# Expert jobs of a hybrid diffusion kernel: the next job's token rows fetched by an indirect DMA in place of gather products

## What is computed

```python
def moe_swiglu(h, w_router, b_router, w_gate, w_up, w_down):
    t = h.reshape(bsz * t_len, dm)
    logits = (t @ w_router).astype(jnp.float32) + b_router.astype(jnp.float32)
    top_v, top_i = lax.top_k(logits, TOP_K)                  # 2 of 8
    top_p = jax.nn.softmax(top_v, axis=-1)
    comb = jnp.sum(jax.nn.one_hot(top_i, N_EXPERTS) * top_p[..., None], axis=1)
    y = jnp.zeros_like(t)
    for e in range(N_EXPERTS):
        y = y + comb[:, e:e + 1] * swiglu(t, w_gate[e], w_up[e], w_down[e])   # width 1408
```

## Time and profile before

| | |
|---|---|
| median of 3 runs | 1898.19 us |
| lowest, highest | 1896.22, 1906.67 us |
| the profiled execution, its own time | 1911.24 us |
| its span, first to last instruction | 1909.3 us |
| PE busy | 1778.1 us, 93% |
| DVE busy | 1130.6 us, 59% |
| ACT busy | 902.9 us, 47% |
| POOL busy | 556.3 us, 29% |
| DMA | 315.33 MB, mean 165 GB/s |
| mean granted clock of PE | 0.97 of 2.4 GHz |

### The profile page before, as it was taken

The page is one execution under the profiler, slowest core; times in us unless marked ns, Lnnn a source line. Parts: engine busy times, 40 slices in busy tenths (PEclk is TensorE's granted clock), DMA queues, the critical chain, the costliest instruction groups (busy, mean ns, idle before and its releaser), DMA issues.

```text
span 1909.3 us, 40982 instructions
## 1 busy us (share of the span) xinstructions
PE 1778.1 (93%) x16558; PEld 1628.1 (85%) x16558; DVE 1130.6 (59%) x1623; ACT 902.9 (47%) x1358; POOL 556.3 (29%) x423
## 2 busy tenths in 40 slices
PE   7898989899999999989988899999899999999996
PEld 6896868799999999989968788999788878888885
DVE  2365688754331111033666885532589888889987
ACT  3335242243344333333441423434567777777765
POOL 1560000265566666656600003656300000000000
PEclk9998989999999999989999999999999999999998
DMA  8446141233423444423571101336388999899880
GB/s 286 153 135 225 48 130 60 82 117 116 154 78 122 133 133 133 125 86 106 162 229 60 33 4 32 111 127 217 133 312 296 297 316 310 308 316 316 291 286 34
DMA packets 225286, 315.33 MB, mean 165 GB/s; under 512 B 15734, under 2 KB 169716, under 8 KB 225012
## 3 DMA queue, kind: packets, MB, share of 16 engines
q1 hardware_dynamic: 217856, 306.22, 48.8%
q10 hardware_dynamic: 7284, 6.97, 1.2%
HBM read 311.05 MB, written 2.10 MB: 164 GB/s over the span
## 4 chain that ended last, share of the span: by engine, by line
PE 78%; DVE 11%; issue 4%; ACT 4%; DMA 1%; ACTq 1%; DVEq 0%; POOL 0%; SPq 0%
PE bank L598 76%; PE bank L595 2%; DVE e_w_rest L186 2%; DVE S L1981 2%; DMA ring<-in_w_ada 1%; ACT e_w_rounded L1354 1%; DVE cvT L1884 1%; DVE hg_rest L1785 1%; DVE St L2033 0%; DVE U L2011 0%; DVE hT L1753 0%; DVE St L2030 0%; DVE hT L1734 0%; DVE tmp L1899 0%; DVE ey_rest L2291 0%
## 5 line engine op out<-in xcount | busy, mean ns | idle before, releaser
L2384 POOL TENSOR_TENSOR weights_rest<-ring,weights_rounded 128x512 fp32r<-128x512 f32 x344 | 467.4, 1362 | 457.7 <-ACT weights_rounded L1317 456.9
L186 DVE TENSOR_TENSOR e_w_rest<-e_raw,e_w_rounded 128x1024 fp32r<-128x1024 f32 (+1 forms) x326 | 353.7, 1132 | 35.0 <-ACT e_w_rounded L1354 33.8
L1317 ACT ACTIVATE weights_rounded<-ring 128x512 fp32r<-128x512 f32 x344 | 215.5, 629 | 335.1 <-PE bank L598 322.3
L1354 ACT ACTIVATE e_w_rounded<-e_raw 128x1024 fp32r<-128x1024 f32 (+1 forms) x327 | 315.2, 989 | 80.8 <-PE bank L598 80.2
L598 PE MATMUL bank<-h_rounded,weights_rounded 128*128 128x384 f32 x688 | 234.4, 341 | 12.4 <-DVE h_rest L1785 4.9
L598 PE MATMUL bank<-h_rest,weights_rounded 128*128 128x384 f32 x688 | 232.2, 338 | 0.0
L598 PE MATMUL bank<-h_rounded,weights_rest 128*128 128x384 f32 x688 | 232.2, 337 | 0.0
L598 PE MATMUL bank<-e_w_rounded,hG_rounded 128*128 128x512 f32 (+1 forms) x432 | 164.5, 381 | 6.7 <-DVE hG_rest L2283 3.5
L598 PE MATMUL bank<-e_w_rest,hG_rounded 128*128 128x512 f32 (+1 forms) x432 | 162.7, 377 | 0.0
L598 PE MATMUL bank<-e_w_rounded,hG_rest 128*128 128x512 f32 (+1 forms) x432 | 162.7, 377 | 0.0
L598 PEld LDWEIGHTS bank<-h_rounded,weights_rounded 128*128 128x128 f32 x688 | 131.1, 191 | 16.7 <-issue 6.0
(11 more groups left out here) (350 smaller groups left out, 3615.4 us busy)
## 6 DMA issues: line engine op xcount, KB each, us to landing
ring<-in_w_ada SPq DMA_DIRECT2D x96, 512.0 KB, 6.2
e_raw<-in_moe_w_down SPq DMA_DIRECT2D x90, 512.0 KB, 4.6
ring<-in_w_in SPq DMA_DIRECT2D x88, 512.0 KB, 4.5
e_raw<-in_moe_w_gate SPq DMA_DIRECT2D x72, 512.0 KB, 5.6
e_raw<-in_moe_w_up SPq DMA_DIRECT2D x72, 512.0 KB, 6.6
e_raw<-in_moe_w_gate SPq DMA_DIRECT2D x36, 384.0 KB, 3.8
e_raw<-in_moe_w_up SPq DMA_DIRECT2D x36, 384.0 KB, 3.9
ring<-in_ffn_w_gate SPq DMA_DIRECT2D x22, 512.0 KB, 4.6
```

The costliest lines, as they stand in the source:

```text
L186: eng.tensor_tensor(wl, e_raw[n % E_RAW][:, 0:kn * w], wr.bitcast(F32), ALU.subtract).then_inc(s("e_rest"), 1)
L1317: a(w_parts[n % NSLOT][0], raw, ACT.Copy).then_inc(*E.up("rounded_ready", *key))
L1354: a(e_w[n % E_PARTS][0][:, 0:kn * w], e_raw[n % E_RAW][:, 0:kn * w], ACT.Copy).then_inc(s("e_rounded"), 1)
L2384: pool.tensor_tensor(wl, raw, wr.bitcast(F32), ALU.subtract).then_inc(*E.up("rest_ready", *key))
```

## The change

The next job's rows are no longer multiplied together on PE. Before the loop POOL adds the two parts of the token rows and stores the sums, 1.5 MB, to device memory (h_rows). In each job, the token numbers ride along with the mixing weights as a second column of wsel; the product with sel gives for each slot its weight and its row number. DVE copies both out of bank 5 (slot_values: rows_at, wnext), and POOL issues an indirect DMA that fetches the 128 rows to hgt. PE waits for it ahead of the transposes behind piece 31.

For this DVE selects earlier, behind the rest of piece 19 (SELECT_AT = 20), and the small product with wsel (slot_rows) moves on PE from before piece 16 to behind piece 20. As the down products overwrite bank 5, PE waits at piece 24 for the copies (e_rows_at). hgt gets a place of its own; the first job still uses gather products. The weight buffers start at a fixed column, 88 further on than before.

```diff
-GATHER_AT, GATHERED_AT = 29, 31
+SELECT_AT, SLOTS_AT, ROWS_AT, GATHERED_AT = 20, 20, 27, 31
...
+E_RAW_AT = 25640
...
+    out["token"] = i[:, None] + P * np.arange(4)[None, :]
...
+            def slot_rows(i):
+                pe.wait_ge(s("e_wsel"), i + 1)
                 for j in range(3):
-                    last = mm(psum[5][:, 0:1], sel[:, j, :].bitcast(F32), wsel[:, j:j + 1], j == 0, j == 2)
-                last.then_inc(s("e_selT_full"), 1)
+                    last = mm(psum[5][:, 0:2], sel[:, j, :].bitcast(F32), wsel[:, j, :], j == 0, j == 2)
+                last.then_inc(s("e_slot_full"), 1)
...
-            turn_gathered(0)
+            turn_gathered(True)
+            slot_rows(0)
...
+                        if n == SLOTS_AT:
+                            slot_rows(i + 1)
...
                     if k0 == 0:
                         pe.wait_ge(s("e_selT"), i * 2 + 2)
+                        pe.wait_ge(s("e_rows_at"), i + 2)
...
-                    if n == GATHER_AT:
-                        pe.wait_ge(s("e_sel"), i + 2)
-                        for h in range(2):
-                            for part in range(2):
-                                gather(h, part)
-                    elif n == GATHERED_AT:
-                        turn_gathered(i + 1)
+                    if n == GATHERED_AT:
+                        pe.wait_ge(s("e_rows_in"), i * 16 + 16)
+                        turn_gathered(False)
...
-                        a(wslot, psum[5][:, 0:1], ACT.Copy).then_inc(s("e_selT"), 1)
+                        act.wait_ge(s("e_rows_at"), i + 1)
+                        a(wslot, wnext, ACT.Copy).then_inc(s("e_selT"), 1)
...
-                e_round(i, done + 4, GATHER_AT + E_PARTS)
-                e_gathered(i + 1)
-                e_round(i, GATHER_AT + E_PARTS, GATHERED_AT + E_PARTS)
+                e_round(i, done + 4, GATHERED_AT + E_PARTS)
...
-            select_weights(lambda at_: slice(at_, at_ + 1))
+            dve.tensor_copy(wsel[:, :, 1], tab("token")[:, 0:3]).then_inc(*E.step())
+            select_weights(lambda at_: slice(at_, at_ + 1)).then_inc(s("e_wsel"), 1)
...
+            def slot_values(i):
+                dve.wait_ge(s("e_slot_full"), i + 1)
+                dve.tensor_copy(rows_at, psum[5][:, 1:2])
+                dve.tensor_copy(wnext, psum[5][:, 0:1]).then_inc(s("e_rows_at"), 1)
+
+            slot_values(0)
...
+                    if c == 2:
+                        e_rests(i, done, SELECT_AT)
+                        dve.wait_ge(s("e_selT_full"), i + 1)
+                        code = dve.value_load(rt_i[0:1, bass.ds(i + 19, 1)], min_val=0, max_val=NCODE - 1)
+                        select_slots(lambda at_: bass.ds(code + at_, 1))
+                        select_weights(lambda at_: bass.ds(code + at_, 1)).then_inc(s("e_wsel"), 1)
+                        done = SELECT_AT
...
-                    if c == 2:
-                        dve.wait_ge(s("e_selT_full"), i + 1)
-                        code = dve.value_load(rt_i[0:1, bass.ds(i + 19, 1)], min_val=0, max_val=NCODE - 1)
-                        select_slots(lambda at_: bass.ds(code + at_, 1))
-                        select_weights(lambda at_: bass.ds(code + at_, 1)).then_inc(s("e_sel"), 1)
+                dve.wait_ge(s("e_selT"), i * 2 + 2)
+                slot_values(i + 1)
                 e_rests(i, done, done + 4)
...
+            pool.wait_ge(s("e_gather"), 2)
+            for j in range(3):
+                pool.tensor_tensor(h_sums[:, j, :], hT_parts[0][:, j, :].bitcast(F32), hT_parts[1][:, j, :].bitcast(F32), ALU.add)\
+                    .then_inc(*E.up("row_summed"))
+                pool.wait_ge(*at("row_summed"))
+                pool.dma_start(h_rows[j * P:(j + 1) * P, :], h_sums[:, j, :]).then_inc(*E.up("rows_stored", by=16))
+            pool.wait_ge(*at("rows_stored"))
+            pool.wait_ge(*at("jobs_ready"))
+            njobs = pool.value_load(rt_i[0:1, 0:1], min_val=NE, max_val=NJOB)
+            with pool.Fori(0, njobs) as i:
+                pool.wait_ge(s("e_rows_at"), i + 2)
+                pool.wait_ge(s("e_hT_full"), i * 2 + 2)
+                pool.sem_inc(s("e_rows_go"), 1)
+                pool.indirect_dma_start(hgt, None, h_rows, bass.IndirectOffsetOnAxis(rows_at, 0))\
+                    .then_inc(s("e_rows_in"), 16)
```

More of the change, by code:

```diff
@@ L94, in tables @@
     return {k: np.asarray(v, np.float32) for k, v in out.items()}
-FIRST = ("ident", "ones", "before", "iota", "code", "eps")
+FIRST = ("ident", "ones", "before", "iota", "code", "token", "eps")
 def table_columns():
@@ L309, in build @@
         htok = cut("htok", o, 3 * DM).rearrange("p (j d) -> p j d", j=3)
-        hT_parts = parts("htoken", DM, 3, o, o + 3 * DM); o += 6 * DM
+        hT_parts = parts("htoken", DM, 3, o, o + 3 * DM)
+        h_sums = cut("h_sums", o, 3 * DM).rearrange("p (j d) -> p j d", j=3)
+        hgt = cut("hgt", o + 3 * DM, DM); o += 6 * DM
         hG = parts("hG", P, KD, o, o + DM); o += 2 * DM
         eprod = cut("eprod", o, DE); o += DE
-        hgt = cut("hgt", used["eprod"][0], DM)
+        hgt0 = cut("hgt0", used["eprod"][0], DM)
         ey = [p_[:, 0, :] for p_ in parts("ey", DM, 1, o, o + DM)]; o += 2 * DM
@@ L316, in build @@
         sel, selT = parts("sel", P, 3, o, o + 3 * P); o += 6 * P
-        wsel = cut("wsel", o, 3); o += 3
+        wsel = cut("wsel", o, 6).rearrange("p (j w) -> p j w", w=2); o += 6
         wslot = cut("wslot", o, 1); o += 1
+        wnext = cut("wnext", o, 1); o += 1
+        rows_at = cut("rows_at", o, 1).bitcast(I32); o += 1
         esig = cut("esig", o, 512); o += 512
@@ L325, in build @@
         fin_row = cut("fin_row", o, DM); o += DM
-        o = (o + 7) // 8 * 8
+        assert o <= E_RAW_AT
+        o = E_RAW_AT
         e_raw = [cut(f"e_raw{i}", o + i * DM, DM) for i in range(E_RAW)]; o += E_RAW * DM
@@ L359, in gsig @@
             return tmp4[3 if i % 8 >= 4 else 0][:, (i % 4) * T:(i % 4 + 1) * T]
+        h_rows = nc.dram_tensor("h_rows", [T, DM], F32, kind="Internal").ap()
         sems = {}
@@ L1140, in gather, with turn_gathered @@
                     last.then_inc(s("e_gather"), 1)
-            def turn_gathered(i):
+            def turn_gathered(first):
                 for h in range(2):
-                    pe.wait_ge(s("e_hgt"), i * 2 + h + 1)
+                    if first:
+                        pe.wait_ge(s("e_hgt"), h + 1)
                     for k in range(4):
-                        last = transpose(psum[h][:, k * P:(k + 1) * P], hgt[:, (4 * h + k) * P:(4 * h + k + 1) * P])
+                        last = transpose(psum[h][:, k * P:(k + 1) * P], (hgt0 if first else hgt)[:, (4 * h + k) * P:(4 * h + k + 1) * P])
                     last.then_inc(s("e_hT_full"), 1)
@@ L1152, in slots @@
                 for j in range(3):
-                    transpose(psum[4][:, j * P:(j + 1) * P], sel[:, j, :].bitcast(F32))
+                    last = transpose(psum[4][:, j * P:(j + 1) * P], sel[:, j, :].bitcast(F32))
+                last.then_inc(s("e_selT_full"), 1)
+            def slot_rows(i):
+                pe.wait_ge(s("e_wsel"), i + 1)
                 for j in range(3):
-                    last = mm(psum[5][:, 0:1], sel[:, j, :].bitcast(F32), wsel[:, j:j + 1], j == 0, j == 2)
-                last.then_inc(s("e_selT_full"), 1)
+                    last = mm(psum[5][:, 0:2], sel[:, j, :].bitcast(F32), wsel[:, j, :], j == 0, j == 2)
+                last.then_inc(s("e_slot_full"), 1)
             def scatter(i, n_):
@@ L1655, in _, with e_gathered @@
             round_tokens(range(2, 6))
-            def e_gathered(i):
+            def e_gathered():
                 for h in range(2):
-                    act.wait_ge(s("e_gather"), i * 2 + h + 1)
-                    a(hgt[:, h * 512:(h + 1) * 512], psum[2 + h][:, :], ACT.Copy).then_inc(s("e_hgt"), 1)
+                    act.wait_ge(s("e_gather"), h + 1)
+                    a(hgt0[:, h * 512:(h + 1) * 512], psum[2 + h][:, :], ACT.Copy).then_inc(s("e_hgt"), 1)
             def e_hG_round(i):
@@ L1668, in e_hG_round @@
                         .then_inc(s("e_hG_rounded"), 1)
-            e_gathered(0)
+            e_gathered()
             act.dma_start(fin_row, dram["final_norm"].rearrange("(o d) -> o d", o=1).broadcast_to([P, DM]))\
@@ L2223, in select_weights @@
                 for j in range(3):
-                    ins = dve.tensor_copy(wsel[:, j:j + 1], rt[:, code(R_CW + 24 * j)])
+                    ins = dve.tensor_copy(wsel[:, j, 0:1], rt[:, code(R_CW + 24 * j)])
                 return ins
@@ L2450, in _ @@
             pool.memset(yacc, 0.0).then_inc(*E.up("zeroed", "yacc"))
+            for k in range(6):
+                pool.wait_ge(*drained("htok", k))
+            s = lambda name: sem(name).h
+            pool.wait_ge(s("e_gather"), 2)
[13 more added lines that the diff above has]
+                    .then_inc(s("e_rows_in"), 16)
```

## The result

| | before | after |
|---|---|---|
| median | 1902.43 us (4 runs) | 1941.85 us (4 runs, 1934.08 to 1944.6) |
| the profiled execution, its own time | 1911.24 us | 1944.6 us |
| its span | 1909.3 us | 1942.7 us |
| mean granted clock of PE | 0.970 | 0.958 |

The kernel before was run again beside the changed one, hence its 1902.43 in place of the 1898.19 ahead. The ratio of the two is 1.0181, with a 95% interval of [1.0148, 1.0215]: slower by 34 us where 16 were forecast. The two medians taken alone lie 39 us apart; all that follows goes by the ratio. The sign is right, the time lies outside the range of 1896 to 1930.

What follows compares the result with a forecast made beforehand. PE was taken to bound the expert jobs, with DVE close behind. Walk +0.5, clock +12.6 and start +3 summed to +16 us, 1914 us against the median of 1898.19, with a range of 1896 to 1930.

Steps and rivals of the forecast that it cites:

- walk of a job: One steady expert job without the clock: -2.77 + 0.7 + 3.0 - 0.88, that is +0.05 us, about +0.5 over nine.
- clock behind the wait: PE at half clock behind the new hole in all nine jobs: 1.4 us per drop, +12.6 us (0 to 15).
- start: Before the loop, POOL's three additions hold up DVE's routing work: 3 us taken, from 0 to 7.
- What bounds the kernel: In the expert jobs PE leads at 55.20 of 56.10 us busy; its savings count only while DVE's results are in time.
- The wait at piece 20: In each job PE waits 0.7 us for remainder 20, which DVE makes after the selection moved forward.
- The wait at piece 24: Before the first down piece PE waits 3.0 us (2.4 to 3.7) for DVE's copies of the slot values.
- The old wait at piece 27: PE's idle of 0.88 us per job behind the old selection was to go, remainder 27 being finished early.
- The first rival: No clock drop behind the 3 us hole; only walk and start remain: +3.5, 1902 us, chance 0.24.
- The term that stood at zero: Moving the weight buffers by 88 columns was to change no load's condition; no cost was put in the sum.
- The late rows: Rival: the fetched rows take more than 11 us and PE waits before their transposes; at 13 us, 1932 us; chance 0.08.
- The gather fully gained: Rival: hole of 2.4 us, no wait at piece 20, steady clock; a job gains 1.25 us, 1887 us; chance 0.06.

Runs made afterwards that it cites:

- the kernel with the padded table: The changed kernel with its token table widened from 4 to 16 columns, moving later tiles by 64 bytes in place of 16: 1928.35 us, ratio 1.0117.
- the filled wait: The changed kernel with twelve matmuls of 512 columns, whose result nobody reads, ahead of PE's wait at piece 24: 1923.92 us, ratio 1.0102.
- bank 2: The changed kernel with the slot product written to bank 2 in place of bank 5 and no wait at piece 24: 1894.67 us, ratio 0.9945.

## Why the prediction was right or wrong

| term | forecast | measured |
|---|---|---|
| walk of a job, without the clock | +0.05, nine times +0.5 | +0.2, nine times +1.4 (the job without a drop, of the kernel with the padded table, 56.26 against 56.10) |
| clock behind the wait | 1.4, nine times 12.6 | 1.6, nine times 14.3 (1.4 by the filled wait) |
| the rest of a job (58.06 - 57.85, without and with the padded table) | none | 0.2, nine times 1.9 |
| start | 3 (0 to 7) | 6.6 |
| everything ahead of the expert part | 0 | 10.2 (the remainder of 34.4) |

**What bounds the kernel: right.** PE sets the pace, and every saved microsecond of PE counted as soon as nothing took its place (bank 2, 2.8 per job).

**The walk of a job: right.** The wait at piece 20 was to be 0.7 and is 0.67. The wait at piece 24 was to be 3.0 and is 3.33 on the weight loads, 3.09 on the matmuls. The cause was the one named, DVE's queue in front of its two copies; these take 0.14 us together where 0.3 was taken. The old wait at piece 27 is gone.

**The clock: right.** The drop came in nine jobs of nine. The price was read off seven slow matmuls behind the hole at 1378.98 as 1.4; the filled wait gives the same 1.4, the one job without a drop 1.6. The first rival (no drop, 0.24) has fallen in the changed kernel, though one job of the padded one shows that it is not a certainty at this length.

**The start: a step that failed.** It was taken at 3 us and measured 6.6. "I take 3, since only the first two meet the chain" was a middle between 0 and 7, taken against the row of z. "Only the first two meet the chain" was wrong: all three did. And in this chain of short, dependent operations the middle was no good choice: an operation of 0.2 us that met an addition of 2.37 was held to its end, and a later one met the next addition. Three such meetings cost 2.2, 2.8 and 1.6 us, 6.6 in all, nearly the three whole additions. The Trainium skill (SBUF — State Buffer, "Who interferes with whom") calls the port that the two engines share an exclusive lock. By that the start would have cost up to the 7, and the trace agrees: DVE's operations end with POOL's. The row of z, 406 ns at least and 1545 at most, is of a longer operation and did not show such a meeting in full; its median was no measure of it.

**The term that stood at zero: the step that failed most.** "Moving the weight buffers by 88 columns changes no load's condition" looked at the buffers only, and only at their loads. The diff also puts 4 columns into the constant table, ahead of nearly all that the trunk works on, and this was never costed. It measured 10 us where the sum had nothing, more than the range had left. The two moves of the kernel before (16 bytes 1.0052, 32 bytes 1.0005) show it without any other part of the change. The difference of the two profiled executions at 1380 us, 9.8 us, would not have shown it alone, since executions of one and the same trunk differ by as much: the kernel moved by 32 bytes reaches that gather at 1361.34 and the unmoved one at 1372.52, both at 334 ns. The size of one instruction decided, and ten runs of the moved kernel against 22 of the unmoved one.

**The late rows (0.08): fallen.** The fetch took 1.07 us on POOL and landed 7.1 us after its issue in the median, more than twice the 3.2 us of the prediction's estimate. But between the issue at 1610.80 and the transposes at 1623.03 lay 12 us, so 5 were to spare. **The gather fully gained (0.06): not in this kernel**, where it needed a hole of 2.4 us and a steady clock; with another bank it came true, at -2.8 per job, and more than that rival had hoped, as the whole hole went.

**Range and chances.** Of the 18 us between the 16 forecast and the 34 measured, 10 are the term at zero, 3.6 the start, and the rest, 4.5, the clock, the walk and the rest of a job. With these at their measured sizes but nothing ahead of the expert part, the sum gives 1902 + 24, inside the range; with the ten as well it lies outside, at 1937, and the median of the runs at 1942. The ten alone on top of the forecast would also have stayed inside, at 1929. The range was built from the terms on the list, and the largest miss was not on it.

## What to carry to other kernels

A product that only has to be picked up should not lie in a bank that others are about to overwrite: here the wait for its reader cost 3 us, and the idleness of PE another 1.4 to 1.6 in half clock. Before costing a diff, list every allocation whose size changes and all that lies behind it; one row of mean durations in an untouched stretch tells whether the shift matters. And work given to an idle POOL wasn't free while DVE had work: here its three additions of 2.37 us cost 6.6 us at the start, and 4.6 where they were put later.

## What was not expected of the hardware

Between 570 and 830 us matmuls of 384 columns took 334 ns with operands at multiples of 32 bytes and 336 to 340 ns when all operands were moved by 16 or 48 bytes. (In other stretches the mean reached 341 ns without any move, as for those of hg_rounded with weights_rounded.) A dense stretch became 1.3% longer (33.28 to 33.70 us), at 8 bytes 1.9% (33.92). Three comparisons with 16 bytes put this at 9 to 12 us of the program, those with 48 and 8 bytes at 14; the mechanism is open. An indirect DMA of 128 rows of 4 KB cost 1.07 us on POOL. It landed 7.1 to 7.2 us after its issue while the engines were 0.9 busy, and in 4.2 at the least. POOL's addition itself took 4.35 us instead of 2.37 where it met DVE's remainders of 128x1024: there both sides paid.
